# Opening of a two-block transformer layer on one core: the halves of the input are made ahead of its norm, and the first projections are scaled as they leave PSUM

## What is computed

```
h    = rms_norm(x, g_pre_mix)            # x * rsqrt(mean(x*x) + eps) * gain, the mean over features
proj = h @ w_in                          # sb q, k, v (512 each), q latent 256, kv latent 128, rope key 32
q    = rms_norm(q_lat, g_q_lat) @ w_q_up;  kv = rms_norm(kv_lat, g_kv_lat) @ w_kv_up
rope on q and on the rope key with cos and sin of positions * inv_freq
stick-breaking attention on sb q, k, v; MLA attention on q, k, v; output projection, conv FFN, ...
block 2: ... memory attention with rms_norm(mem, norm_mem) @ w_mem_kv ...
```

## Time and profile before

| | |
|---|---|
| runs, us | 1007.25, 1006.81, 1019.7; median 1007.25 |
| the profiled execution, us | 1007.77 |
| its span, first to last instruction, us | 1006.0 |
| TensorE busy | 907.8 us, 90% of the span |
| VectorE, ScalarE, POOL busy | 678.2, 509.2, 318.1 us (67%, 51%, 32%) |
| mean granted TensorE clock | 0.938 of 2.4 GHz |

### The profile page before, as it was taken

How to read it: one execution, slowest core, us unless ns; L and a number is a source line. 1 busy time by engine, 2 the same in 40 slices (tenths; PEclk the granted TensorE clock), 3 DMA queues, 4 the chain that set the end, 5 groups by cost and what they waited for, 6 DMA issues and landing times.

```text
span 1006.0 us, 16923 instructions
## 1 busy us (share of the span) xinstructions
PE 907.8 (90%) x6718; PEld 861.8 (86%) x6718; DVE 678.2 (67%) x984; ACT 509.2 (51%) x926; POOL 318.1 (32%) x150
## 2 busy tenths in 40 slices
PE   4996879998879897988999788999998899999998
PEld 3985769998879886977889678988898899999998
DVE  7857742877666766276779998783668466566573
ACT  5477345743444445665664554255544454444440
POOL 3653103111221212423455751121243222222220
PEclk8997779999999999899999989799899899999999
DMA  5734005344445455534346361222154355666651
GB/s 181 272 114 139 21 2 158 116 135 127 147 143 168 138 162 163 171 103 129 127 157 186 106 228 45 83 82 88 63 147 147 126 156 180 189 189 182 183 161 43
DMA packets 54078, 137.18 MB, mean 136 GB/s; under 512 B 6000, under 2 KB 24816, under 8 KB 53872
## 3 DMA queue, kind: packets, MB, share of 16 engines
q1 hardware_dynamic: 54000, 136.11, 43.3%
HBM read 135.03 MB, written 1.05 MB: 135 GB/s over the span
## 4 chain that ended last, share of the span: by engine, by line
PE 62%; DVE 20%; ACT 9%; issue 8%; DMA 1%; DVEq 0%; SPq 0%; ACTq 0%
PE PROD L576 11%; PE PROD L577 11%; PE PROD L578 11%; ACT whi L1012 5%; DVE wlo L1491 4%; DVE YC L1774 3%; PE SC L717 3%; PE OP L761 3%; PE PROD L638 2%; DVE RS L1499 2%; PE SC L576 2%; PE TP L578 2%; PE TP L577 2%; PE TP L576 2%; PE SC L577 2%
## 5 line engine op out<-in xcount | busy, mean ns | idle before, releaser
L559 POOL TENSOR_TENSOR wlo<-raw,whi 128x1024 fp32r<-128x1024 f32 x124 | 314.3, 2542 | 664.3 <-ACT whi L1012 664.3
L576 PE MATMUL PROD<-HA,whi 128*128 128x256 f32 x1096 | 320.9, 293 | 22.8 <-DVE HA L1519 7.1
L577 PE MATMUL PROD<-HA,wlo 128*128 128x256 f32 x1096 | 316.2, 288 | 0.0
L578 PE MATMUL PROD<-HA,whi 128*128 128x256 f32 x1096 | 315.9, 288 | 0.0
L1491 DVE TENSOR_TENSOR wlo<-raw,whi 128x1024 fp32r<-128x1024 f32 x128 | 185.5, 1453 | 153.0 <-ACT whi L1012 152.8
L1012 ACT ACTIVATE whi<-raw 128x1024 fp32r<-128x1024 f32 x252 | 261.9, 1050 | 44.9 <-PE PROD L578 23.9
L576 PEld LDWEIGHTS PROD<-HA,whi 128*128 128x128 f32 x1096 | 216.8, 198 | 26.3 <-DVE HA L1519 7.9
L577 PEld LDWEIGHTS PROD<-HA,wlo 128*128 128x128 f32 x1096 | 217.0, 198 | 0.6 <-issue 0.5
L578 PEld LDWEIGHTS PROD<-HA,whi 128*128 128x128 f32 x1096 | 216.5, 198 | 0.0
L1905 DVE SCALAR_TENSOR_TENSOR CY<-U,CV,CY 128x255 f32<-128x255 f32 (+29 forms) x120 | 67.3, 633 | 0.2
L576 PE MATMUL SC<-ACTS,whi 128*128 128x256 f32 x176 | 52.8, 300 | 16.2 <-DVE ACTS L1519 8.1
(11 more groups left out here) (316 smaller groups left out, 1761.0 us busy)
## 6 DMA issues: line engine op xcount, KB each, us to landing
raw<-stream SPq DMA_DIRECT2D x208, 512.0 KB, 3.8
raw<-stream SPq DMA_DIRECT2D x136, 128.0 KB, 2.4
raw<-stream SPq DMA_DIRECT2D x8, 384.0 KB, 3.2
raw<-stream SPq DMA_DIRECT2D x8, 256.0 KB, 3.1
X<-xT SPq DMA_DIRECT2D x2, 512.0 KB, 5.0
E<-memT SPq DMA_DIRECT2D x1, 1024.0 KB, 5.8
out<-X SPq DMA_DIRECT2D x8, 128.0 KB, 2.0
PX<-pT SPq DMA_DIRECT2D x1, 256.0 KB, 3.8
```

The costliest lines, as they stand in the source:

```text
L559: nc.gpsimd.tensor_tensor(wlo[:, n % NSPLIT, :], raw[:, n % NRAW, :], whi[:, n % NSPLIT, :].bitcast(F32), ALU.subtract).then_inc(lo_pool, 1)
L576: nc.tensor.matmul(dst, wh, hi, start=start, stop=False, skip_group_check=True)
L577: nc.tensor.matmul(dst, wl, hi, start=False, stop=False, skip_group_check=True)
L578: last = nc.tensor.matmul(dst, wh, lo, start=False, stop=stop, skip_group_check=True)
```

## The change

- The input is split without its norm: `early_high` writes HA's high half as X times the gain, VectorE the low half, both straight from X. The sum of squares goes between `lat` 1 and `lat` 2. `scaled` and the normed halves of h1 are gone.
- The reciprocal goes to RSF, and VectorE multiplies each of `lat`, `sbq`, `sbk` (12 outputs) by it on the way out of PSUM (`early_out`), in place of ScalarE's copies and the rope straight from PSUM. The squares of the latents are now made from Y. ScalarE only keeps its tiles going (`follow`).
- For `sbv` the factor must stand on partitions: after the memory's sum TensorE turns RSF by two transposes ("h1T", a bank and a place in the order of its own), VectorE copies a column of each half to RST and scales `sbv` by it on the way out.
- The angles move on VectorE behind the `early_out` of `sbk` 2, ahead of the memory's norm; the `early_out` of `sbk` 3 stands behind the memory's `scaled`; the key's rope and its copy come behind the memory's low halves. The sines move on ScalarE behind the memory's high halves; the first table that it loads is that of the root.
- Tiles 0 and 1 are split by VectorE, no longer by POOL. On SP tile 0 is issued ahead of X, and the positions behind tile 4.
- `lat` and "h1" may use the bank OP too: `lat` 0 and 3 are in bank 0, `lat` 1 in 1, "h1" in 2, `lat` 2 in OP; the first product into OP later waits for `lat` 2's release.

```diff
 def lo_on_vector(n):
-    return n % 3 == 2 if n not in FFN_TILES else n % 3 != 0
+    return n < 3 or (n % 3 == 2 if n not in FFN_TILES else n % 3 != 0)
@@ outputs
-    out = [("stat", "h1")]
-    out += [("lat", m) for m in range(4)]
+    out = [("lat", 0), ("lat", 1), ("stat", "h1"), ("lat", 2), ("lat", 3)]
...
-    out += [("sbk", m) for m in range(4)] + [("stat", "mem"), ("sbv", 0), ("sbv", 1)]
+    out += [("sbk", m) for m in range(4)] + [("stat", "mem"), ("stat", "h1T"), ("sbv", 0), ("sbv", 1)]
@@ banks
+EARLY_OUTS = {("stat", "h1")} | {("lat", m) for m in range(4)}
-        _k = min(range(NBANK + (_o in FFN_OUTS)), key=lambda k: _seen[k])
+        _k = min(range(NBANK + (_o in FFN_OUTS | EARLY_OUTS)), key=lambda k: _seen[k])
@@ sync
-            sp.dma_start(Y[:, 1, :].bitcast(I32), pos).then_inc(pos_in, 16)
             sp.dma_start(CV[:, :], consts).then_inc(consts_in, 16)
-            for i in range(2):
-                sp.dma_start(X[:, 4 * i:4 * i + 4, :], xT[:, 4 * i:4 * i + 4, :]).then_inc(x_in[i], 16)
             for n in range(NTILES):
...
+                if n == 0:
+                    for i in range(2):
+                        sp.dma_start(X[:, 4 * i:4 * i + 4, :], xT[:, 4 * i:4 * i + 4, :]).then_inc(x_in[i], 16)
+                if n == 4:
+                    sp.dma_start(Y[:, 1, :].bitcast(I32), pos).then_inc(pos_in, 16)
@@ tensor
-            stat("h1", [SQ[:, c, :] for c in range(8)])
             for m in range(4):
+                if m == 2:
+                    stat("h1", [SQ[:, c, :] for c in range(8)])
                 fm("lat", m, HA, SP0["h1"] if m == 0 else None)
...
             stat("mem", [SQ[:, c, :] for c in range(8)])
+            pe.wait_ge(rs_ready, RT["h1"] + 1)
+            dst = begin(("stat", "h1T"))
+            for qt in range(QT):
+                last = nc.tensor.transpose(dst[:, qt * P:(qt + 1) * P], RSF[:, qt * P:(qt + 1) * P], ident[:, :])
+            last.then_inc(y_done, 1)
@@ scalar
+            warm(ACT.Sqrt)
             weights(1)
             act.wait_ge(consts_in, 16)
+            act.wait_ge(x_in[0], 16)
+            for c in range(4):
+                early_high(c)
+            squares("h1", 0, X[:, 0, :])
+            squares("h1", 1, X[:, 1, :])
+            act.wait_ge(x_in[1], 16)
+            for c in range(4, 8):
+                early_high(c)
+            weights(2)
+            for c in range(2, 6):
+                squares("h1", c, X[:, c, :])
+            weights(3)
+            for c in range(6, 8):
+                squares("h1", c, X[:, c, :])
+            weights(4)
             root("h1", D)
...
             for m in range(3):
-                wait_product(act, ("lat", m))
-                src = product(("lat", m))[:, 0:S]
-                squares(None, m, src)
-                nc.scalar.activation(Y[:, 4 + m, :], src, ACT.Copy).then_inc(free(("lat", m)), 1)
+                wait_freed(act, ("lat", m))
+                squares(None, m, Y[:, 4 + m, :])
                 ahead(("lat", m))
+            def follow(o):
+                wait_product(act, o)
+                ahead(o)
...
             normed_high(HB, "mem", 8, "norm_mem_2")
+            act.wait_ge(angles, 2)
+            nc.scalar.activation(SIN[:, :], SIN[:, :], ACT.Sin).then_inc(sincos, 1)
+            nc.scalar.activation(COS[:, :], COS[:, :], ACT.Sin).then_inc(sincos, 1)
@@ vector
+            def early_out(o, dst):
+                wait_product(dve, o)
+                nc.vector.tensor_tensor(dst, product(o)[:, 0:S], RSF[:, :], ALU.mult).then_inc(free(o), 1)
+                ahead(o)
+            weights(1)
+            dve.wait_ge(consts_in, 16)
+            for c in range(8):
+                low(HA, "h1", c, X[:, c, :], CV[:, COL["g_pre_mix"] + c:COL["g_pre_mix"] + c + 1])
+            weights(3)
+            inverse_root("h1", dst=RSF)
+            weights(NSPLIT)
+            for m in range(4):
+                early_out(("lat", m), Y[:, 4 + m, :])
+            for m in range(2):
+                early_out(("sbq", m), QS[:, m, :])
+            inverse_root("qlat")
...
+            for m in range(2, 4):
+                early_out(("sbq", m), QS[:, m, :])
+            for m in range(3):
+                early_out(("sbk", m), KS1[:, m, :])
...
+            inverse_root("mem")
+            scaled("mem", MEMX, 8)
+            early_out(("sbk", 3), KS1[:, 3, :])
+            normed_low(HB, "mem", "mem", 8, "norm_mem_2")
+            turned = ("stat", "h1T")
...
+            dve.wait_ge(sincos, 2)
+            link(nc.vector.tensor_scalar(SIN[:, :], SIN[:, :], CV[:, COL["sign"]:COL["sign"] + 1], None, ALU.mult))
+            link(rope(Y[:, 7, :], KM[64:96, 0, :], 0))
...
+                nc.vector.tensor_scalar(VS1[:, qt, :], product(o), RST[:, qt:qt + 1], None,
+                                        ALU.mult).then_inc(free(o), 1)
```

More of the change, by code:

```diff
@@ L188 @@
         Y_COUNT[_o] = _c
-PLAIN_STATS = ("gk", "gv", "kcT", "vc", "lnmean")
+PLAIN_STATS = ("h1T", "gk", "gv", "kcT", "vc", "lnmean")
+EARLY_OUTS = {("stat", "h1")} | {("lat", m) for m in range(4)}
 FFN_OUTS = {(n, m) for n in ("up", "up2") for m in range(2 * FC)} | {("stat", "memk0"), ("stat", "memk1")}
 BANK, PREV, FREE_COUNT = {}, {}, {}
-_last, _seen, _c = {}, [-NBANK + i for i in range(NBANK)] + [0], [0] * 8
+_last, _seen, _c = {}, [-NBANK - 1 + i for i in range(NBANK + 1)], [0] * 8
 for _i, _o in enumerate(OUTS):
@@ L271 @@
 RT = {n: i for i, n in enumerate(RT_ORDER)}
[L272 removed]
+TN0 = bases([("ql", 1), ("kvl", 1), ("mem", 4), ("xn2", 4)])
 SPLITS = [("h1", 8), ("ql", 2), ("kvl", 1), ("mem", 8), ("o", 8), ("ffn", 8), ("a", FC), ("p", 2), ("ph", 8),
@@ L313, in program @@
         valid = sb("valid", [P, QT])
+        RST = sb("RST", [P, QT])
         eps = sb("eps", [P, 2])
@@ L686, in sb_pv @@
                 pe.wait_ge(sb_a, u + 1)
+                if u == 0:
+                    wait_freed(pe, ("lat", 2))
                 o_begin(("sb", u))
@@ L1092, in _, with early_high @@
             act.wait_ge(masks, 1)
[L1093 to L1097, removed]
+            warm(ACT.Sqrt)
             weights(1)
             act.wait_ge(consts_in, 16)
-            act.wait_ge(angles, 2)
-            nc.scalar.activation(SIN[:, :], SIN[:, :], ACT.Sin).then_inc(sincos, 1)
-            nc.scalar.activation(COS[:, :], COS[:, :], ACT.Sin).then_inc(sincos, 1)
+            def early_high(c):
+                high(HA, c, X[:, c, :], CV[:, COL["g_pre_mix"] + c:COL["g_pre_mix"] + c + 1])
+            act.wait_ge(x_in[0], 16)
[13 more added lines that the diff above has]
+            weights(4)
             root("h1", D)
-            normed_high(HA, "h1", 8, "g_pre_mix")
             nc.scalar.activation(hbp[:, :], CV[:, COL["b_ple_gate"]:COL["b_ple_gate"] + 8], ACT.Copy,
@@ L1120, in copy_out @@
                 ahead(o)
-            copy_out(("sbq", 0), QS[:, 0, :])
-            copy_out(("sbq", 1), QS[:, 1, :])
+            follow(("sbq", 0))
+            follow(("sbq", 1))
             root("qlat", 2 * P)
@@ L1128, in _ @@
             high(HL, 2, SQ[:, 2, :], CV[:, COL["g_kv_lat"]:COL["g_kv_lat"] + 1])
-            copy_out(("sbq", 2), QS[:, 2, :])
-            copy_out(("sbq", 3), QS[:, 3, :])
-            copy_out(("sbk", 0), KS1[:, 0, :])
+            follow(("sbq", 2))
+            follow(("sbq", 3))
+            follow(("sbk", 0))
             act.wait_ge(mem_in, 16)
@@ L1623, in _ @@
                 nc.vector.tensor_scalar(dst[:, :], dst[:, :], -3.1415925, None, ALU.max).then_inc(angles, 1)
-            inverse_root("h1")
-            scaled("h1", X, 8)
-            weights(2)
-            normed_low(HA, "h1", "h1", 8, "g_pre_mix")
-            weights(NSPLIT)
+            inverse_root("mem")
[3 more added lines that the diff above has]
+            turned = ("stat", "h1T")
+            wait_product(dve, turned)
@@ L1629, in _ @@
+            nc.vector.tensor_copy(RST[:, :].unsqueeze(2), product(turned)[:, 0:S].rearrange(
+                "p (q n) -> p q n", q=QT)[:, :, 0:1]).then_inc(free(turned), 1)
             dve.wait_ge(sincos, 2)
             link(nc.vector.tensor_scalar(SIN[:, :], SIN[:, :], CV[:, COL["sign"]:COL["sign"] + 1], None, ALU.mult))
-            for m in range(3):
-                ahead(("lat", m))
-            o = ("lat", 3)
-            wait_product(dve, o)
-            rope(product(o), KM[64:96, 0, :], 0).then_inc(free(o), 1)
@@ L1636, in _ @@
-            wait_freed(dve, o)
-            nc.vector.tensor_copy(KM[64:96, 1:8, :], KM[64:96, 0:1, :].to_broadcast((32, 7, S)))
-            ahead(o)
-            ahead(("sbq", 0))
-            ahead(("sbq", 1))
-            inverse_root("qlat")
-            scaled("ql", Y[:, 4:6, :], 2)
-            normed_low(HL, "ql", "ql", 2, "g_q_lat")
-            inverse_root("kvlat")
-            scaled("kvl", Y[:, 6:7, :], 1, base=2)
-            low(HL, "kvl", 0, SQ[:, 2, :], CV[:, COL["g_kv_lat"]:COL["g_kv_lat"] + 1], base=2)
@@ L1647, in _ @@
```

(14 more changed lines are left out.)

9 lines of the change are left out of this document (6 added, 3 removed).

## The result

Twenty executions of each kernel: 1019.91 us median after (1013.58 to 1022.58), 1008.91 before (1001.61 to 1019.7). The ratio is 1.0104, with a 95% interval of 1.0082 to 1.0126: the change costs some 10.5 us where 5.0 was forecast, and the median lies 0.9 above 1019, the top of the range. The profiled execution took 1015.66 us, its span 1013.9.

A forecast was written before the change was run, and what follows sets the result against it. TensorE bounds the kernel (62% of the chain), except VectorE and ScalarE from 3.95 to 20.06 us. Terms -6.7 + 8.8 + 1.3 + 2.4 - 0.8 = +5.0 on 1007.77 gave 1012.8 us, range 1005 to 1019.

The forecast's parts named there:

- stall at `lat` 3: Before `lat` 3: TensorE waits 2.9 us for `lat` 0's bank, freed late by VectorE.
- the angles: On VectorE after `sbk` 2: 18 operations take 6.6 us plus 3.0 of blocking by POOL, bounds 0 and 3.8.
- `sbv` at the low clock: After the 8 us wait `sbv` starts at the low clock, costing 2.4 us, bounds 1.5 and 3.4.
- the start: Opening: `lat` 0 starts at 8.5 us instead of 20.06, with X split as its halves land.
- the 16.2: Small sums to the end of `sbk` 2: 16.2 us as before, so `sbk` 2 ends at 50.9, 6.7 ahead.
- All else shifts: Behind `sbv` and the rope: the later bank order is the same, and the rest merely shifts, with no term of its own.
- The clock at `lat` 3: In the stall before `lat` 3 the clock may fall: price 0 or 2.4 us, 1.3 taken.
- The halves of X near 7.1: Opening: with tile 0 issued ahead, the halves of X land near 7.1 and 8.4 us.
- Rival 3: Tile 11 tie with POOL: latents' norm 2.4 later, TensorE loses 1.9 ahead of `sbk` 1; 1017 us, chance 0.21.
- 1 (no blocking): At the angles and tile 5: POOL doesn't block VectorE where said and the clock keeps; 1007 us, chance 0.20.
- 2 (the gain reaches the end): Behind `sbv`: VectorE's own backlog decides, so the 6.7 and 0.8 gained count; 1000 us, chance 0.04.
- 4 (clock stays low until the rope): After the 8 us wait: clock low until VectorE's rope, some 20 us of work at half speed; 1028 us, chance 0.03.

The follow-up runs named there:

- the repeat: The changed kernel run once more with nothing altered, as a control; ratio to the kernel before 1.009 (1.0063 to 1.0118).

## Why the prediction was right or wrong

The direction and the mechanism were right: `lat` early, a stall at `lat` 3, the angles slowed by POOL, TensorE idle ahead of `sbv` for the release of `sbk` 3, `sbv` at the low clock. The result lies within 2%, as 0.96 of the chances had it. The size was half of the measured one, and the top of the range (1019) 0.9 us too low. The steps that failed are terms of the sum: the start (1.5 short), the 16.2 carried over from the small sums to `sbk` 2 (1.7 short), the angles (0.5 short), and "All else shifts", which put what comes behind the rope at nothing, where 4.5 us were lost in this profile and 1.5 in the repeat. Point by point:

- **Right.** The stall at `lat` 3, 2.9 said, 2.62 measured. Reciprocal and scaling of the memory, 4.25 said, 4.3. TensorE idle 8 ahead of `sbv`: 8.77. `sbv` at the low clock, +2.4: 13.0 us instead of 11.1, so 1.9. From the first to the third Z 8.9 instead of 9.7, the 0.8 that I took off for rope beside POOL.
- **The clock at `lat` 3**, 1.3 said between 0 and 2.4: `lat` 3 to the small sums took 10.17 for 8.9 + 1.3. That it fits is luck. 1.3 was a middle between two cases; where the clock fell it cost 1.3 to 1.5 and not 2.4, and in one of nine profiles it didn't fall.
- **"The halves of X near 7.1"** was late by 1.8: X landed 7.2 to 8.1 us behind its issue and not 4.6 to 5.4. I moved the landing by the issue alone, as if 512 KB ahead of it on the queue cost 0.8. Part of the 1.8 is scatter: `lat` starts 0.5 to 1.8 later than I said in the eight profiles with this code. At the small sums 1.5 was left.
- **"From the small sums at 41.42 to the end of `sbk` 2 at 57.63 it was 16.2"**: it was 17.9. I carried the stretch over. VectorE's way from tile 11 to the end of the latents' norm, "from 35.6 to 43.7", took 10.1 us (38.85 to 48.92) and not 8.1, since tile 11's low half met POOL (2.90); so `sbq` 2's bank, and `sbk` 1 behind it, came late, and TensorE waited 0.81 at `sbk` 0 and 0.69 at `sbk` 1. Rival 3 had this mechanism, with 1.9 for it and 0.21 of the chances; moving tile 11 gave back 2.0. Part of it is a tie, as rival 3 had it: the low half took 1.26 in the run without the wait at `lat` 3, and in the kernel before 1.25 in one profile and 2.99 in another. So the 16.2 was itself one draw, and the other was 17.5.
- **The angles, 6.6 + 3.0.** 10.16 measured, 3.66 of it blocking by the run without POOL there. Two operations were held (1.94 and 2.35), inside my bounds of 0 and 3.8. The Trainium skill's page "SBUF — State Buffer", section "Who interferes with whom", has the two engines exclude each other for a whole instruction, and lets a VectorE instruction with at most one SBUF input, outside the 2-port modes, go free. These rows agree, and so do the `early_out`s, whose other input is in PSUM: none took over 0.43 us in any run, beside POOL or not.
- **The sum.** 1.5 (start) + 1.7 (tile 11) + 0.5 (angles) put `sbv` at 70.7 and not 67.0, as measured; 0.5 comes back in `sbv`, by its smaller clock price. So the marks say +8.2 at the third Z where I said +5.0. The whole times say +10.5, interval 8.3 to 12.7. The rest lies between the third Z and the first FFN output, where the profile of after stands at +12.7 and the repeat at +9.1, at a granted clock of 0.75 and 0.83 against 0.87. The profile of before, against which I summed, had an opening 1.6 us slower than the same code in another run; the profile of after was 0.6 slower at the third Z than its repeat.
- **Rivals.** 1 (no blocking) falls with the two held operations, 2 (the gain reaches the end) with `sbv`'s wait, 4 (clock stays low until the rope) with 0.88 granted at 74 to 78 us, in `sbv` itself. But a piece of rival 2 was true: with the wait taken away, VectorE's own backlog sets the first Z.

What stays open: why the stretch from 100 to 180 us is granted 0.74 to 0.89 over the profiles, 0.74 and 0.83 for equal code among them, and how much of this follows from the opening and how much is chance. There is only one profile of the unchanged kernel before.

## What to carry to other kernels

On an engine that works in order, the instruction that frees a bank goes ahead of everything that nobody waits for yet; an output that moves to another engine moves into that engine's queue, and what stands there ahead of it is the price, not the 0.42 us of the copy. A gain at the start is worth nothing until each later release keeps up, so follow two or three marks along the kernel. Where executions scatter by more than the effect, set marks beside the ratio, and carry them on until the code has been the same for a while: here the third Z missed up to 4.5 us that the first FFN output showed. A stretch carried over from one profile is one draw: look for a second profile of the same code. Put new work of VectorE where POOL is quiet, or where VectorE waits anyway: there the same 18 operations cost nothing that the marks show.

## What was not expected of the hardware

- A transfer's landing depends on what was issued just ahead, and scatters: 4.6 to 5.4 us for X with no tile ahead, 7.2 to 8.1 behind a tile of 512 KB; over all profiles 4.2 to 6.4 (three of them) and 5.9 to 8.1 (eleven). With X first the tile came some 3 us later.
- Equal code differs: the kernel before took 1001.61 to 1019.7, and the kernel with `sbk` 3 ahead of the angles was granted 0.74 and 0.83 between 100 and 180 us in its two profiles, and gave 1.0105 and 1.0056 in its two groups of executions.
- The clock fell in a wait of 2.62 us at `lat` 3 (0.78 granted at 28 to 34), in eight of the nine profiles with this wait and in none without it; it costs 1.3 to 1.5 us on top of the wait. In the ninth 1.00 was granted.
